# A 1-core transformer kernel: where the operands of its split float32 matmuls start in on-chip memory

## What is computed

```
def swiglu(x, w_gu, w_down):                       # four times, D_FF = 2816
    g, u = jnp.split(x @ w_gu, 2, axis=-1)
    return (jax.nn.silu(g) * u) @ w_down

mix = jnp.concatenate([o_tok, o_mem], -1) @ w_out  # twice, 1024 x 1024
proj = h @ w_in                                    # HGRN mixer, 1024 x 5120

def peer_ffn(h, w_q, sub_keys, u_tab, v_tab):      # twice, 16384 experts, 8 heads, top 16
    q = (h @ w_q)...                               # scores, top_k, gates
    act = gelu(einsum('thkd,td->thk', u_tab[idx], h))
    return einsum('thk,thkd->td', gate * act, v_tab[idx])
```

## Time and profile before

| | us |
|---|---|
| three runs, median (lowest, highest) | 3134.91 (3128.31, 3135.98) |
| profiled execution | 3136.78 |
| its span, first to last instruction | 3135.1 |

### The profile page before, as it was taken

The page is one execution under the profiler, slowest core; times in us unless marked ns, Lnnn a source line. Parts: engine busy times, 40 slices in busy tenths (PEclk is TensorE's granted clock), DMA queues, the critical chain, the costliest instruction groups (busy, mean ns, idle before and its releaser), DMA issues.

```text
span 3135.1 us, 52364 instructions
## 1 busy us (share of the span) xinstructions
PE 3039.0 (97%) x18414; PEld 2686.9 (86%) x18414; DVE 2320.9 (74%) x4339; ACT 1529.3 (49%) x2659; POOL 114.9 (4%) x132
## 2 busy tenths in 40 slices
PE   8998999999999998899999999999999999999998
PEld 7876887887578897799999988887799999988887
DVE  7866887786576688689889955555579989975555
ACT  5435543543454465444544445553645544445554
POOL 0010111001010000000000000000100000000000
PEclk9999999999999999999999999999999999999999
DMA  8762686876135542145544455555335544455554
GB/s 325 281 256 87 250 299 231 291 281 224 54 126 187 175 167 98 54 162 182 181 142 139 141 181 193 191 192 196 125 135 181 181 155 141 139 170 194 193 191 152
DMA packets 124976, 567.82 MB, mean 181 GB/s; under 512 B 13872, under 2 KB 14000, under 8 KB 97328
## 3 DMA queue, kind: packets, MB, share of 16 engines
q1 hardware_dynamic: 108864, 504.41, 46.2%
q0 software_dynamic: 15264, 58.73, 5.5%
q10 hardware_dynamic: 720, 3.00, 0.2%
HBM read 565.03 MB, written 1.05 MB: 181 GB/s over the span
## 4 chain that ended last, share of the span: by engine, by line
PE 86%; DVE 5%; ACT 2%; issue 1%; DMA 0%; DVEq 0%; ACTq 0%
PE turn L353 47%; PE gather L353 38%; ACT arena L1359 1%; PE turn L866 0%; DVE arena L2610 0%; ACT hT L1359 0%; ACT L1359 0%; PE gather L661 0%; DVE arena L2469 0%; DVE arena L2301 0%; DVE ring_low L2143 0%; DVE arena L2296 0%; DVE arena L2057 0%; DVE arena L2418 0%; DVE x_rows L2059 0%
## 5 line engine op out<-in xcount | busy, mean ns | idle before, releaser
L1359 ACT ACTIVATE dense<-ring 128x1024 fp32r<-128x1024 f32 x544 | 576.1, 1059 | 388.0 <-PE gather L353 347.4
L2632 DVE TENSOR_TENSOR ring_low<-ring,dense 128x1024 fp32r<-128x1024 f32 x544 | 662.9, 1219 | 79.5 <-ACT dense L1359 77.4
L353 PE MATMUL turn<-expert_src_high,ring_low 128*128 128x256 f32 x2496 | 708.4, 284 | 0.0
L353 PE MATMUL turn<-expert_src_high,dense 128*128 128x256 f32 x2304 | 665.9, 289 | 1.2 <-DVE expert_src_low L2134 1.2
L353 PE MATMUL turn<-expert_src_low,dense 128*128 128x256 f32 x2304 | 653.5, 284 | 0.0
L353 PE MATMUL gather<-dense 128*128 128x512 f32 x2048 | 631.7, 389 | 2.1 <-DVE ring_low L2632 2.1
L353 PE MATMUL turn<-rounded 128*128 128x512 f32 x1408 | 504.3, 402 | 0.0
L353 PEld LDWEIGHTS turn<-expert_src_high,ring_low 128*128 128x128 f32 x2496 | 480.4, 192 | 0.0
L353 PEld LDWEIGHTS gather<-dense 128*128 128x128 f32 x2048 | 384.5, 188 | 82.4 <-DVE ring_low L2632 2.9
L353 PEld LDWEIGHTS turn<-expert_src_high,dense 128*128 128x128 f32 x2304 | 443.5, 192 | 1.8 <-issue 1.8
L353 PEld LDWEIGHTS turn<-expert_src_low,dense 128*128 128x128 f32 x2304 | 444.0, 193 | 0.0
(11 more groups left out here) (259 smaller groups left out, 3885.6 us busy)
## 6 DMA issues: line engine op xcount, KB each, us to landing
ring<-tiles_in SPq DMA_DIRECT2D x544, 512.0 KB, 3.3
ring<-stream SPq DMA_DIRECT2D x205, 1024.0 KB, 5.4
arena<-ada_in POOLq DMA_DIRECT2D x96, 512.0 KB, 4.4
arena<-tables_in POOLq DMA_DIRECT2D x6, 1024.0 KB, 7.3
arena<-keys_in SPq DMA_DIRECT2D x2, 1024.0 KB, 7.9
arena<-c_in POOLq DMA_DIRECT2D x3, 512.0 KB, 5.6
hT<-x_in SPq DMA_DIRECT2D x1, 1024.0 KB, 4.8
x_rows<-rows_in ACTq DMA_DIRECT2D x1, 1024.0 KB, 21.4
```

The lines of the kernel that those rows point to most:

```text
L353: return nc.tensor.matmul(out, lhsT, rhs, start=start, stop=stop, skip_group_check=True)
L1359: return nc.scalar.activation(out, in_, func, **kw)
L2632: V.tensor_tensor(tile_words(t, ring_low).bitcast(R32), tile_words(t), tile_high[:, t % AHEAD, :], ALU.subtract).then_inc(S("tile_low"), 1)
```

## The change

Starting addresses alone are changed. The instructions of all engines and their order stay as they are.

- 8 words (32 bytes) are left out after `x_rows`, and 24 words (96 bytes) after `hidden`. So `hT` with `expert_src_low`, and `gated` and `hidden` with `expert_src_high`, start 32 bytes past a multiple of 128; what follows them keeps its place relative to such a multiple.
- In `rounded`, 8 words are left out ahead of `src`, so `src_high` and `src_low` start 32 bytes past a multiple, and the hidden parts ahead of them stay.
- `aligned` rounds up to 32 words, 128 bytes, so `out_rest`, `hin_high2`, `hin_high3` and all of `hg_high` start on a multiple.

```diff
--- before.py
+++ after.py
@@ -54,6 +54,9 @@
 SLOTS = 6
 HALF = PIECE // 2
 
+LINE = 32
+APART = 8
+
 TILE_SLOTS = 6
 Q_TILES = 2 * PEER_HEADS
 U_TILES = Q_TILES
@@ -188,6 +191,7 @@
         arena = sb("arena", [P, NKEYS * T])
         arena_at = nc.sbuf_base - 4 * NKEYS * T
         x_rows = sb("x_rows", [P, TT, DM])
+        sb("apart", [P, APART])
         hT = sb("hT", [P, KC, T])
         out_rows = hT[:, :, :].rearrange("p (t c) w -> p t (c w)", t=TT)
         expert_src_low = nc.alloc_sbuf_tensor_at("expert_src_low", [P, KC, T], F32,
@@ -196,6 +200,7 @@
         hidden = sb("hidden", [P, 4, T])
         expert_src_high = nc.alloc_sbuf_tensor_at("expert_src_high", [P, KC, T], F32,
                                                   offset=nc.sbuf_base - 4 * KC * T)
+        sb("apart_end", [P, LINE - APART])
         params = sb("params", [P, N_PARAMS])
         consts = sb("consts", [P, N_CONSTS])
         mod = sb("mod", [P, 12 * KC])
@@ -251,12 +256,13 @@
 
 
 
-        n_parts = 4 * HALF + 2 * KC * T + 8 * T
+        n_parts = 4 * HALF + 8 * T + APART + 2 * KC * T
         rounded = nc.alloc_sbuf_tensor_at("rounded", [P, n_parts], F32, offset=arena_at + 4 * NKEYS // 2 * T)
         parts = Place(0, n_parts, rounded)
         w_high = parts.take(4, HALF)
         hid_high = parts.take(4, T)
         hid_low = parts.take(4, T)
+        parts.take(APART)
         src = parts.take(2, KC, T)
         src_high, src_low = src[:, 0, :, :], src[:, 1, :, :]
 
@@ -328,7 +334,7 @@
         peer_keys = carve(BEFORE * T - 16 * NKEYS, 16, NKEYS)
 
         def aligned(at):
-            return (at + 7) // 8 * 8
+            return (at + LINE - 1) // LINE * LINE
 
         def over(name, at, *shape):
             return nc.alloc_sbuf_tensor_at(name, [P, *shape], F32, offset=arena_at + 4 * at)
```

## The result

The changed kernel takes 3108.0 us (median of 4 runs, 3103.62 to 3109.25), the kernel before 3135.39 in its runs beside them (3128.31 to 3135.98). The ratio is 0.992, 95% interval [0.9905, 0.9936]: 27 us faster. The forecast was 3075, 62 us faster. The direction and the stages were right, and the size was more than twice too large.

The account below looks back on a forecast made before the run. TensorE, busy 97% of the span, was taken as the bound, so time follows the matmuls' start distance. Terms of -38, -20, -2.5 and -1.6 summed to -62 us, from 3136.8 to 3075 us; stated range 3012 to 3170.

Parts of the forecast that it names:

- At best the floor, -11 ns each: Expert projections, best bound: start distance falls from 120 to about 109 ns per 256-column matmul, -76 us.
- Part (1): Expert projections, sources moved to 32 bytes: 114.5 ns a matmul, -5.5 ns x 6912 = -38 us.
- Part (2): Feed-forward projections, sources moved to 32 bytes: half of the excess goes, -14 ns x 1408 pairs = -20 us.
- the 28: Feed-forward projections: a pair takes 353 ns, 28 ns over an assumed floor of 325 ns.
- Part (3): HGRN projections, sources to 32 and weights to 0: 288 matmuls from 120 and 288 from 117.5 to 114.5 ns, -2.5 us.
- Part (4): Output projections, `out_rest` and six `hg_high` halves from 64 to 0: 48 + 24 triples at -22 ns, -1.6 us.
- Parts (5) and (6): Full fp32 matmuls with `hT`, and VectorE, ScalarE and DMA work hidden behind TensorE: no change in time.
- Full release: Rival: both reads never meet, every distance falls to the floor, -123 us, 3015 to 3030 us; chance 0.17.
- No effect: Rival: excess stems from the instruction switch, or 32 behaves as 0; only part (4) remains, 3134 us; chance 0.14.
- The price of an offset moving operand: Rival "slower": each projection matmul with an offset source pays up to 7.4 ns, +76 us, 3213 us; chance 0.26.

Follow-up runs that it names:

- al_only: The kernel before with only the new rounding of arena places to 128 bytes, sources at 0; 3133.1 us, ratio 0.9998.
- both32: The changed kernel with `ring`, `dense`, `ring_low` and `w_high` also moved by 32 bytes, so sources and these weights both at 32; 3133.43 us, ratio 1.0005.
- s64: The changed kernel with the projections' sources 64 bytes past a multiple of 128 instead of 32; 3110.5 us, ratio 0.9921.
- quarter_load: The kernel before with 32 of the 128 stationary columns in the expert projections, the other products left out; 3106.41 us, one run.
- w32: The changed kernel with `ring`, `dense`, `ring_low` and `w_high` at 32 bytes and the sources back at 0; 3120.66 us, ratio 0.9959.

## Why the prediction was right in sign and wrong in size

- **"At best the floor, -11 ns each".** This step failed, and with it the size. I took the floor of a reduced-type matmul from full fp32, 109 ns. The Trainium skill gives nearly the same (TensorE: Matmul & The Clock Gate, Back-to-back issue gap: an isolated gap of N / 2.4 + 2.5 ns, by which 109.2 is an estimate for 256 columns). No stretch of any run here reaches that with this type. The reduced type goes at 0.443 ns a column. The floor is 113.3 for 256 columns, 680 for a triple of 512 and, as their sum, 340 for a pair; no run shows a pair at 340. It stood in the rows: `out_first` triples take 680, 113.3 for each 256 columns. I read that as an excess of "11 ns" there too, when it was the floor itself. Six or seven of the 11 ns did exist: 120 - 113.3.
- **Part (1), -5.5 ns a matmul.** It measured -19.5 us over both stages rather than -38. Working from the right floor, and half of the excess as I did, gives -3.3 x 6912 = -23. The reason that I gave for going below HGRN's 117.5 (single distances of 113, and three loads apart rather than two) was wrong too: single distances alternate within a pattern. In ns, one after the other:

```
before, loop over u_tab tiles     120 120 120 120 120 120
after, the same loop              117 117 116 117 117 116
after, the loop with the gates    118 120 113 116 117 120 114 116
before, feed-forward pairs        233 117 241 120 236 113
after, feed-forward pairs         229 118 228 119 228 118
```

  A shortest distance of 113 is the floor showing once in a pattern, not a level that the mean can reach. HGRN's mean, 2.5 ns x 6912 = -17 us, was the better estimate.
- **Part (2), -14 ns a pair.** It measured -6.6 x 1408 = -9.3 us. The excess over the right floor was 353.3 - 340 = 13.3, and half of it went: the "half" held, the 28 did not.
- **Part (3), -2.5 us.** A half with `hg_high` went from 120.0 to 117.8 ns a matmul, and one with `hin_high` stayed at 117.8: -0.6 us for 288 matmuls. al_only, with all operands at 0, has 120.0 in every half.
- **Part (4), -1.6 us.** Nothing came of it. `out_rest` was to reach 680 and reached 696, and `out_first` rose from 680 to 696. The stationary operand `expert_src_high` had moved to 32 while the weights stood at 0; of that I had given bounds (-1 and +3 us) and no term in the sum. al_only, with both at 0, has 680 for both.
- **Parts (5) and (6), nothing.** Right, as far as the remainder of about 1 us tells. TensorE waits 12.8 us for `ring_low` in the pairs, much as before.
- **The rivals.** Full release can't be: its 109 ns don't exist for this type. No effect falls by 27 us. The price of an offset moving operand falls by both32. What fed it, `out_rest` at 702, was again a matter of relative starts: its 64 bytes against the other operand's 0.

With the right floor and the same "half" the sum is -23 - 9.4 - 0.6 = -33, 3104 us, within 6 us of the profiled 3109.25. That is worked out afterwards. The "half" had no reason beyond its nearness to the HGRN rows, and that it held for the pairs was luck.

**What stays open.** Why equal starts with whole loads always give 120, why 96 bytes do too, and what in the two reads meets. What selects the pattern when several are possible: an order of the three matmuls, a pause before a run, or fewer accesses of the other engines and DMAs beside it were not tried. Whether the 113.3 that s64 has for a moment with whole loads can be had throughout. What distances s64 has in its faster executions, of which there is no trace.

## What to carry to other kernels

Take the floor of a matmul stream from matmuls of the same type in the same trace, here the widest ones, which take longer (227 ns) than a load shows (188). When a stream of reduced-type matmuls of 256 columns stands above it, try starting its moving operand 16 or 32 bytes further past a multiple of 128 than its stationary one (the other way round gave about half), and leave 512-column streams, which are at the floor with equal starts, as they are. Expect half of the excess, here 2.6% of those matmuls' time and 0.8% of the kernel, and count over long runs of starts: single distances mislead, and one execution may not stand for the median, as in s64.

## What was unexpected of the hardware

- The reduced type moves a column in 0.443 ns (226.7 ns for 512, 113.3 for 256 at best), 6% above one clock at 2.4 GHz. Full fp32 stands 1% above whole clocks (215.5 against 213.3).
- The load of the next tile nearly always starts 2 to 4 ns behind the start of the matmul that it runs beside, at 113 as at 120 ns. The patterns differ without it.
- The distances fall into patterns of mostly 113.3, 116.7, 117.8 or 120.0 ns on average, some of which last a whole loop. The same loop can run in one of them at its first stage and in another at its second (118 and 120 ns in quarter_load).
- 512-column triples lose 16 ns when two of their three stationary operands start 32 bytes past the moving ones (680 to 696). 256-column matmuls gain 1.7 from such a distance (w32) and 3.1 with the moving operand 32 past the stationary one.
- Most of the spread between runs goes with the mean granted clock, some 2.3 us for each 0.001 (3126.46 us at 0.992, 3152.73 at 0.981).
